# The last RMSNorm of a hybrid encoder block: three of its four token tiles split between GpSimd and ScalarE

## What is computed

```
x = x + merged @ w_out                       # attention and convolution branches
x = x + hier_moe(rmsnorm(x, g_ffn), ...)     # 64 experts, two for each token
return rmsnorm(x, g_final)

def rmsnorm(x, g):                           # over the 1024 channels of a token
    y = x * rsqrt(mean(x * x) + 1e-6)
    return y * g
```

## Time and profile before

| what | value |
|---|---|
| median of 3 runs | 1396.9 us (1395.78 to 1397.3) |
| the profiled execution | 1396.18 us |
| its span, first to last instruction | 1394.2 us |
| outside the span | 1.98 us |
| busy: PE, DVE, ACT, POOL | 85%, 26%, 15%, 13% |
| the chain that ended last: DMA, PE, DVE, ACT | 48%, 42%, 4%, 2% |

### The profile page before, as it was taken

How to read it: one execution, slowest core, us unless ns; L and a number is a source line. 1 busy time by engine, 2 the same in 40 slices (tenths; PEclk the granted TensorE clock), 3 DMA queues, 4 the chain that set the end, 5 groups by cost and what they waited for, 6 DMA issues and landing times.

```text
span 1394.2 us, 14854 instructions
## 1 busy us (share of the span) xinstructions
PE 1182.7 (85%) x4987; PEld 542.4 (39%) x4987; DVE 363.5 (26%) x697; ACT 209.3 (15%) x453; POOL 186.3 (13%) x245
## 2 busy tenths in 40 slices
PE   4999988999979999999987787877877877877771
PEld 3878766744453333333322222222222222222220
DVE  4799454342245322222100000000000000000004
ACT  3133324430110000010010000010010010000002
POOL 2355343000000101000101001001001001000100
PEclk9999999999989999999999999999999999999996
DMA  5341320125244999999999999999999999999974
GB/s 208 106 129 62 111 71 33 52 98 211 90 181 190 373 404 414 415 422 411 402 424 425 424 423 426 424 422 426 424 424 426 419 418 423 415 423 425 418 324 186
DMA packets 58370, 435.77 MB, mean 313 GB/s; under 512 B 10512, under 2 KB 10541, under 8 KB 26090
## 3 DMA queue, kind: packets, MB, share of 16 engines
q1 hardware_dynamic: 52176, 429.21, 74.8%
q0 software_dynamic: 5312, 5.28, 1.1%
q10 hardware_dynamic: 858, 0.95, 0.2%
HBM read 429.10 MB, written 18.36 MB: 321 GB/s over the span
## 4 chain that ended last, share of the span: by engine, by line
DMA 48%; PE 42%; DVE 4%; ACT 2%; issue 2%; SPq 0%; ACTq 0%; POOL 0%; POOLq 0%; DVEq 0%
DMA sb_weights<-in_w_exp_up 46%; PE ps_proj L1276 11%; PE ps_proj L1496 8%; PE ps_proj L1465 5%; PE ps_scores L1513 4%; PE ps_proj L1264 4%; PE ps_proj L1424 4%; PE ps_proj L1317 2%; DMA sb_weights<-in_w_exp_down 1%; DVE sb_x L1225 1%; DMA sb_rb_sb<-in_rel_bias 1%; PE ps_scores L1331 1%; PE ps_aT L1505 1%; ACT sb_scratch L692 1%; DVE sb_scratch L1165 0%
## 5 line engine op out<-in xcount | busy, mean ns | idle before, releaser
L1496 PE MATMUL ps_proj<-sb_weights,sb_scratch 128*64 128x512 f32 x1984 | 471.7, 628 | 75.2 <-DMA sb_weights<-in_w_exp_up 73.7
L1496 PEld LDWEIGHTS ps_proj<-sb_weights,sb_scratch 128*64 128x64 f32 x1984 | 165.8, 144 | 374.0 <-issue 372.1
L1513 PE MATMUL ps_scores<-sb_weights,sb_scratch 128*64 128x512 f32 x992 | 228.5, 597 | 21.8 <-ACT sb_scratch L774 21.8
L1165 DVE TENSOR_TENSOR sb_scratch<-sb_scratch,ps_proj 128x256 f32<-128x256 f32 x62 | 26.1, 421 | 642.9 <-ACT sb_scratch L772 642.9
L585 POOL TENSOR_TENSOR sb_tick<-sb_tick 1x1 f32<-1x1 f32 x62 | 11.3, 183 | 1002.8 <-ACT sb_scratch L779 785.4
L1276 PE MATMUL ps_proj<-sb_hT_r,sb_weights_r 128*128 128x512 f32 x512 | 128.5, 405 | 2.7 <-POOL sb_weights_r L563 2.7
L1513 PEld LDWEIGHTS ps_scores<-sb_weights,sb_scratch 128*64 128x64 f32 x992 | 67.0, 136 | 145.6 <-issue 109.5
L1276 PEld LDWEIGHTS ps_proj<-sb_hT_r,sb_weights_r 128*128 128x128 f32 x512 | 98.0, 194 | 31.0 <-issue 10.1
L772 ACT ACTIVATE sb_scratch<-ps_proj 128x256 f32<-128x256 f32 x62 | 23.8, 383 | 535.5 <-PE ps_proj L1496 535.5
L563 POOL TENSOR_TENSOR sb_weights_r<-sb_weights,sb_weights_r 128x1024 fp32r<-128x1024 f32 x36 | 86.0, 2402 | 78.8 <-ACT sb_weights_r L647 77.8
L779 ACT ACTIVATE sb_scratch<-ps_scores 128x512 f32 (+1 forms) x62 | 37.0, 597 | 268.2 <-PE ps_scores L1513 268.2
(11 more groups left out here) (240 smaller groups left out, 745.5 us busy)
## 6 DMA issues: line engine op xcount, KB each, us to landing
sb_weights<-in_w_exp_down SPq DMA_DIRECT2D x62, 2048.0 KB, 14.6
sb_weights<-in_w_exp_up SPq DMA_DIRECT2D x62, 2048.0 KB, 14.9
sb_weights<-in_w_exp_gate SPq DMA_DIRECT2D x62, 2048.0 KB, 14.7
sb_weights<-in_w_in SPq DMA_DIRECT2D x9, 2048.0 KB, 7.9
sb_x<-in_x SPq DMA_DIRECT2D x8, 512.0 KB, 9.1
sb_weights<-in_w_out SPq DMA_DIRECT2D x2, 2048.0 KB, 10.6
sb_weights<-expert_rows SPq DMA_DIRECT2D x4, 1024.0 KB, 8.0
sb_weights<-in_w_conv_pw SPq DMA_DIRECT2D x1, 2048.0 KB, 7.7
```

The source lines that it names most:

```text
L1496: last = mm(ps_gu[g * BLK:(g + 1) * BLK, :].rearrange("p (a n) -> p a n", a=2), hTb[:, c, half * BLK:(half + 1) * BLK], weights[:, slice(6 ...
L1513: last = mm(ps_y[g * BLK:(g + 1) * BLK, :], actT[:, j, half * BLK:(half + 1) * BLK], weights[:, place(parity, 4 + half), 2 * j + g, :], st ...
```

## The change

For the token tiles 0, 1 and 2 the last scaling is taken from VectorE. GpSimd multiplies the tile by the final weights as soon as the expert sums are in it (`zg = x * g_fin`, into a part of `work`), and ScalarE multiplies the product by the reciprocal root and writes it back to x (`scale_z`). VectorE keeps the sums, the four reciprocals (`inverse`) and the whole of the last scaling of tile 3. SP waits for ScalarE's `scaled` for the first three stores and for VectorE's `fin_ready` for the last.

```diff
+        zg = work[:, D:T * D].rearrange("p (t d) -> p t d", d=D)
@@ SP
             for t in range(T):
-                sp.wait_ge(fin_ready, t + 1)
+                if t < T - 1:
+                    sp.wait_ge(scaled, t + 1)
+                else:
+                    sp.wait_ge(fin_ready, 1)
                 sp.dma_start(out[0, t * P:(t + 1) * P, :], x[:, t, :]).then_inc(out_done, 16)
@@ GpSimd, after the last scatter
+            pool.wait_ge(in_gfin, 16)
+            for t in range(T - 1):
+                pool.wait_ge(z_ready, t + 1)
+                pool.tensor_tensor(zg[:, t, :], x[:, t, :], g_fin[:, :], ALU.mult).then_inc(zg_ready, 1)
@@ ScalarE
+            def scale_z(t):
+                act_e.wait_ge(zg_ready, t + 1)
+                act_e.wait_ge(rstd_ready, t + 1)
+                act_e.activation(x[:, t, :], zg[:, t, :], ACT.Copy, scale=rstd3[:, t:t + 1]).then_inc(scaled, 1)
+
             for t in range(T):
                 ...
                 act_e.activation(rms3[:, t:t + 1], ssq3[:, t:t + 1], ACT.Sqrt, bias=eps_col).then_inc(z_rms, 1)
+                if t:
+                    scale_z(t - 1)
@@ VectorE
-            def final_norm(t):
+            def inverse(t):
                 dve.wait_ge(z_rms, t + 1)
-                link(dve.reciprocal(rstd3[:, t:t + 1], rms3[:, t:t + 1]))
-                dve.scalar_tensor_tensor(out=x[:, t, :], in0=x[:, t, :], scalar=rstd3[:, t:t + 1], in1=g_fin[:, :],
-                                         op0=ALU.mult, op1=ALU.mult).then_inc(fin_ready, 1)
+                dve.reciprocal(rstd3[:, t:t + 1], rms3[:, t:t + 1]).then_inc(rstd_ready, 1)

             dve.wait_ge(in_gfin, 16)
             for t in range(T):
                 add_experts(t)
-                if t >= 2:
-                    final_norm(t - 2)
-            final_norm(T - 2)
-            final_norm(T - 1)
+                if t:
+                    inverse(t - 1)
+            inverse(T - 1)
+            dve.wait_ge(rstd_ready, T)
+            dve.scalar_tensor_tensor(out=x[:, T - 1, :], in0=x[:, T - 1, :], scalar=rstd3[:, T - 1:T], in1=g_fin[:, :],
+                                     op0=ALU.mult, op1=ALU.mult).then_inc(fin_ready, 1)
```

More of the change, by code:

```diff
@@ L379, in block_kernel @@
         in_gfin, in_y = sem("in_gfin"), [sem(f"in_y{t}") for t in range(T)]
+        zg_ready, rstd_ready, scaled = sem("zg_ready"), sem("rstd_ready"), sem("scaled")
         z_ready, z_sq, z_rms, fin_ready, out_done = sem("z_ready"), sem("z_sq"), sem("z_rms"), sem("fin_ready"), sem("out_done")
```

## The result

| | before | changed |
|---|---|---|
| median (8 runs each) | 1395.68 us | 1400.86 us |
| lowest to highest | 1393.55 to 1397.3 | 1398.34 to 1402.44 |
| the profiled execution | 1396.18 us | 1399.62 us |
| its span | 1394.2 us | 1397.4 us |
| first sum starts | 1375.44 | 1374.32 |

The ratio is 1.0043, with a 95% interval of 1.0029 to 1.0056: the changed kernel is slower by 4.0 to 7.8 us (the two medians are 5.2 apart). The forecast was 1401.2 us, slower with a chance of 0.80.

What follows compares the result with a forecast made beforehand. VectorE was taken to bound the last 16 us. The terms -1.39 + 0.2 + 6.2 - 1.16 + 0.74 = +4.6 us gave 1400.8 on the profiled time, 1401.5 on the median; forecast 1401.2 us, range 1398.2 to 1403.2.

Steps and rivals of the forecast that it cites:

- steps 1 and 2: VectorE's end stretch: scaling 0 leaves ahead of sum 3, -1.39 us; two reciprocals come between the sums, +0.2 us.
- sum 3: Tile 3's expert sum on VectorE: claimed to end at 1391.99 us, where it ended at 1386.98.
- step 3: VectorE's sums of tiles 1 to 3: each GpSimd product holds a pair's second instruction, 2.07 us three times, +6.2 us.
- the other turn: At VectorE's sums: GpSimd gets in ahead of a pair's first instruction, 2.3 us per product, three times 6.9.
- step 5: Behind sum 3: tile 3's square, root, reciprocal and scaling stand open, 3.03 us instead of 4.19, so -1.16 us.
- step 6: ScalarE's scalings of tiles 0 to 2: 1.05 us each, tile 2's ending at 1394.46, before VectorE's end at 1395.02.
- step 7: At the last stores: issued 0.56 us apart, so the last waits for the one ahead, +0.74 us.
- The rival without blocking: At VectorE's sums: GpSimd reads beside VectorE without holding it, -1.3 us in all, 1394.9 us; chance 0.09.
- The rival in which VectorE keeps its turn throughout: At the sums: GpSimd gets in only where VectorE idles, +3.7 us with the stores, 1399.9 us; chance 0.08.

Runs made afterwards that it cites:

- e1: The changed kernel without GpSimd's three products, ScalarE scaling x itself (final weights left out for tiles 0 to 2): ratio 0.9989 to the kernel before, tail 17.63 us.
- e3: The kernel before with GpSimd's three products added beside it, their result unused: ratio 1.0048 to the kernel before, tail 24.82 us.
- e9: The changed kernel with sums against PSUM, two GpSimd products and tile 2 scaled by VectorE: ratio 0.9998 to the kernel before, timed again 0.9988.
- e8: The changed kernel with sums against PSUM and the first load of expert rows split in two halves: ratio 0.9997 to the kernel before.
- e2: The changed kernel with each GpSimd product replaced by a memset of the same place, ScalarE scaling x itself: tail 17.61 us.
- e4: The changed kernel with x copied to PSUM beforehand, so each sum has one SBUF and one PSUM input: ratio 0.9996 to the kernel before.

## Why the prediction was right

Its sum was +4.6 us; the tail grew by 4.32, and the timed runs say 4.0 to 7.8, with the medians 5.2 apart. By its own steps:

1. Scaling 0 out, reciprocals in (steps 1 and 2). e1 gives both together with the wait for the first root: sum 3 ends 10.67 us after the start where it was 11.54, so -0.87; the forecast's terms for that case were -1.39 + 0.2 + 0.3 = -0.89. The 0.3 is seen as 0.31, and the products hide it in the changed kernel, as was said.
2. The products (step 3): 2.07 each were forecast, 1.96 measured. The first instruction of each pair kept its turn and the second was held, as worked out from the 192 to 198 us stretch; e3 shows the other turn, at 2.12, forecast as 2.3 (2.35 by the times that the step gives). The term was 0.3 too large over three. Two thirds of that come from one reading of the earlier trace rows: the instruction that was held there was compared with 0.68 us, which is line 945, another operation. Line 906 itself takes 0.75 where nothing holds it, so what VectorE has done by the time GpSimd ends is 0.20 and not 0.13, and its held instruction ends 1.28 - 0.20 = 1.08 after the product and not 1.15. (In rows 7 the instructions are line 938's, and there 0.13 stands.) The rest is the half step towards a product of 2.40, which took 2.34 here. Line 906 without a hold, in the kernel before:

```profile
204.20 0.75 DVE L906 SCALAR_TENSOR_TENSOR sb_scratch<-sb_scratch,sb_small 128x512 f32<-128x512 f32 x1
```

3. Sum 3 should end 5.0 later, and ended 4.63 later (16.17 us after the start against 11.54).
4. The open square and root (step 5): 3.02 us from sum 3 to the end of the last scaling, forecast 3.03. In e9 1.32 us of this wait are put to use.
5. ScalarE's scaling (step 6) takes 1.13 and not 1.05 us. A scale from a column of SBUF goes with it, which the row that I took it from doesn't have. The kernel before shows a like step: a 128x512 copy out of PSUM takes 0.69 us with such a column (line 653) and 0.60 without (line 701). That makes it the likely cause; it was not tried apart.
6. The stores (step 7): +0.74 forecast, +0.86 measured, and e9 shows that it is the queue. The bunching was tighter, 0.47 and not 0.56 apart, for the reason of point 5; with 0.47 the step's own rule gives 1.3 - 0.47 = 0.83.
7. Not forecast: the profiled execution is 2.22 us longer than its span, where it was 1.98. The kernels with GpSimd's or ScalarE's new work mostly show 2.1 to 2.4 (e8 1.93), the ones without 1.8 to 2.0. What these 0.2 us are stays open.

The rival without blocking falls with the changed kernel's own sums at 3.24 us, and holds where its condition is met (e2, e4): e1's 17.63 is its 1.3 less, to 0.2 us. The rival in which VectorE keeps its turn throughout falls with each second instruction of a pair: it was ready and had to stand. The Trainium skill (SBUF — State Buffer, Who interferes with whom) held in both of its halves: reads of GpSimd conflict with VectorE's second SBUF input, and writes do not.

That the absolute time came within 0.4 us of the median is partly luck. The start of the end moves by 5.7 us over the profiles. The forecast also stood on a time before of about 1396.6, and the median of eight runs is 1395.68: a base 0.9 too high made up for a difference of the medians 0.6 larger than forecast. Inside the sum, too, products forecast 0.3 too dear stand against a store forecast 0.1 too cheap. What was forecast well is the difference.

## What to carry to other kernels

Before work is moved from VectorE to GpSimd, look at where VectorE's operands lie: with two SBUF inputs, a GpSimd instruction that reads SBUF cost VectorE its whole time less 0.4 us here (less 0.2 where GpSimd came first), so where VectorE is the bound and has its next instruction ready, giving away 1.28 us for 2.34 can only lose. One input in PSUM, filled while VectorE is idle, makes the same move free. And when an offload shortens a serial end, check that the last two stores don't come out together: here 0.86 us of the gain went there, and came back when the freed engine took the tile before the last in its own idle time.

## What the runs showed of the hardware that was not expected

- The hold grows with GpSimd's time, with the same offset for three durations and two operations: 1.06, 1.27 and 2.34 us hold VectorE for 0.65, 0.88 and 1.96. This is for a GpSimd instruction that waited for its turn; the one that came first (e3) held VectorE for 2.12 of its 2.35.
- A GpSimd copy of 128x1024 with one SBUF input conflicts just as the product with two, while a memset of the same size, 0.95 us, doesn't at all.
- VectorE's `scalar_tensor_tensor` of 128x1024 takes 1.28 us whether its second input and its output are in SBUF or in PSUM (1281 and 1278 ns for 4 each).
- Two loads of 512 KB in place of one of 1024 KB brought the next tile's rows to 8.13 us after the first issue, where they landed about 7.4 after it before; 0.47 of the difference is that their own load was issued later.
